# A relative-bias table: spread by DMA through memory before, turned by TensorE matmuls now

## The chip, the core and the metric

One core of one Trainium2 chip runs the whole program. The metric is the time of one execution on the device, in microseconds (us). The kernel before took 2122.17 us (median of three runs, 2119.29 to 2123.08).

## The reference

The reference computes two blocks of layers on 256 tokens and 256 context tokens of width 1024, all in float32. The first block has two layers with attention and a mixture of 32 experts each, the second block a dilated attention and a state-space layer. The change touches only the attention of the first block's second layer, in which 256 tokens stand in a grid of 4 rows of 64 columns, with 16 heads of 64 numbers. A query sees the 4 rows and 16 columns near its own, and gets a bias that depends on the row offset and the column offset:

```python
bias = rel_bias[:, row_off][:, :, col_off].transpose(0, 2, 1, 3)
s_loc = jnp.einsum('bhqd,bhiqjd->bhqij', qr, kw) * C_SCALE + bias
s_ctx = jnp.einsum('bhqd,bhkd->bhqk', qr, kc_h) * C_SCALE
s = jnp.concatenate([s_loc.reshape(B, C_HEADS, GRID_W, n_loc), s_ctx], axis=-1)
p = jax.nn.softmax(s, axis=-1)
```

`rel_bias` holds 16 heads x 15 row offsets x 31 column offsets. The kernel scores every query against all 256 local keys and 256 context keys, and adds a table to the local part: the bias where the key column is in the query's window, and -1e30 where it is not.

## The kernel before

The five engines run one program each, in an order written out by hand, and wait for each other on semaphores. The order of SyncE (SP) is a list, the ring: every weight matrix comes in pieces of 2 MB into five slots of the tile `RG` (with one or two more slots in the tile `AR` while the experts run). SP goes through the list in order, waits until the work that read a slot before is done, and issues the load (L3181). A copy that stands in SP's program ahead of a piece delays that piece.

The stages around the change run so. After the first expert stage the rows come back (`z_load` on ScalarE's queue), VectorE joins them, and `pe_odd_begin` transposes them with matmuls against a diagonal (L2021); ScalarE and VectorE write the transposed and modulated tokens to `HT` (L2041, L2069). Then `pe_odd` projects the first half of the heads: part c=0 is Q (four banks, 256 columns, L2099), part c=1 is K (four banks, 512 columns, L2099), part c=2 is V (four banks, 512 columns, L2101). Each instruction in the program is two MATMUL records in the trace, since float32 goes in two passes. ScalarE empties banks 0 to 3 (L2108, L2110, L2112). After that `odd_done` waits for the last V bank and for the bias table, and the attention begins (L814 are the scores), with the second half of the projection between its units.

The bias table is `BT`, 16 heads x 384 columns on 128 partitions: partition q (and q+64 for the odd grid rows, shifted by 64 columns) is a query column, and the columns are six row offsets x 64 key columns. Partition q needs the table's row read from an offset that falls as q rises, so it can't be loaded with one forward stride. Before, `sp_bias_spread` makes 16 copies from memory to memory, one for each head (L2119), into `OBD` with 64 rows of 448 numbers for each head, each row reversed in its start; they stand in SP's program ahead of piece `("ada", 0, 6)`, in the first layer's projection. Then `sp_bias` loads the two halves of `BT` (L2126) ahead of piece `("odd", 2, 1)`, and VectorE adds the mask `NM` in eight instructions (L2149).

## Time and profile before

| what | value |
|---|---|
| median of 3 runs | 2122.17 us |
| the profiled execution | 2122.17 us |
| its span on the chip | 2120.3 us |
| TensorE (matmul) busy | 1955.7 us, 92% |
| VectorE / ScalarE / GpSimd busy | 647.4 / 370.5 / 322.0 us |
| data moved by DMA | 584.22 MB, mean 276 GB/s |
| chain that ended last | TensorE 65%, DMA 22%, VectorE 5% |

The span is the time between the first and the last instruction of the execution; 1.9 us lie around it. "Busy" says how long an engine had something to do, not that it was waited for. The chain that ended last is followed back from the last instruction, from each to what released it: what stands in it had no slack. A wait that isn't in it costs nothing.

### The profile page before, as it was taken

The numbers are of one execution on the slowest core, as the hardware profiler recorded it, in microseconds if no ns is written. First come the engines' busy times: TensorE is split into PE (matmuls) and PEld (weight loads), VectorE is DVE, ScalarE is ACT, GpSimd is POOL, SyncE is SP. The second block draws the span as 40 slices with busy tenths as digits, with TensorE's granted clock in tenths as the row PEclk, the third lists the DMA queues.
The fourth block names the chain that finished last, engine by engine and source line by source line (L and its number), as shares of the span: only waits on it lengthen the run. The fifth ranks groups of instructions, "written<-read, shape, count | busy, mean of one in ns | idle before, by whom it ended". The sixth has DMA issues, their size and how long they took to land.

```text
span 2120.3 us, 34138 instructions
## 1 busy us (share of the span) xinstructions
PE 1955.7 (92%) x14829; PEld 1223.9 (58%) x14829; DVE 647.4 (31%) x1508; ACT 370.5 (17%) x821; POOL 322.0 (15%) x264
## 2 busy tenths in 40 slices
PE   5999999999999969999999988988879989989998
PEld 4566575555555445546555444444457677665884
DVE  1234382222222232115331111111136031037752
ACT  3133320000000011114310000000021130042131
POOL 0125412000000000115210000000120060040120
PEclk8999999999999999999999999999989999999999
DMA  9563299999999989317399999999964423427221
GB/s 361 151 208 122 88 383 393 427 427 426 427 424 426 427 327 283 111 40 279 140 383 426 426 423 427 426 422 426 393 240 143 146 80 125 153 78 201 81 92 60
DMA packets 131760, 584.22 MB, mean 276 GB/s; under 512 B 19082, under 2 KB 32490, under 8 KB 106896
## 3 DMA queue, kind: packets, MB, share of 16 engines
q1 hardware_dynamic: 113216, 550.26, 66.0%
q10 hardware_dynamic: 12272, 25.26, 3.3%
q0 software_dynamic: 6112, 6.39, 0.9%
q8 instruction: 122, 2.00, 0.4%
q14 instruction: 38, 0.31, 0.0%
HBM read 572.29 MB, written 23.22 MB: 281 GB/s over the span
## 4 chain that ended last, share of the span: by engine, by line
PE 65%; DMA 22%; DVE 5%; issue 3%; POOL 2%; ACT 2%; SPq 1%; POOLq 0%; DVEq 0%; ACTq 0%
DMA RG<-in_moe_w 20%; PE banks L1545 12%; PE banks L2527 8%; PE banks L1570 5%; PE banks L2099 4%; PE banks L2529 4%; PE banks L1093 4%; PE banks L1521 3%; PE banks L684 3%; PE banks L2101 3%; PE banks L2728 3%; PE banks L2939 2%; POOL AR L921 2%; PE banks L814 2%; PE banks L842 1%
## 5 line engine op out<-in xcount | busy, mean ns | idle before, releaser
L1545 PE MATMUL banks<-RG,HT 128*64 128x256 f32 x3616 | 426.6, 389 | 34.6 <-DMA RG<-in_moe_w 32.7
L1545 PEld LDWEIGHTS banks<-RG,HT 128*64 128x64 f32 x3616 | 250.1, 134 | 218.1 <-DMA RG<-in_moe_w 55.0
L1775 POOL DMA_INDIRECT y_rows<-AR x64 | 63.6, 994 | 871.0 <-DVE AR L1584 870.1
L1554 DVE TENSOR_TENSOR AR<-AR,banks 128x256 f32<-128x256 f32 x64 | 38.6, 603 | 484.3 <-ACT AR L1550 433.1
L1570 PE MATMUL banks<-RG,AR 128*64 128x512 f32 x752 | 171.7, 598 | 3.1 <-DVE AR L1563 3.1
L2527 PE MATMUL banks<-HT,RG 128*128 128x256 f32 x768 | 168.0, 380 | 0.8 <-ACT HT L553 0.8
L2527 PEld LDWEIGHTS banks<-HT,RG 128*128 128x128 f32 x768 | 145.4, 190 | 22.8 <-issue 2.4
L1550 ACT ACTIVATE AR<-banks 128x256 f32<-128x256 f32 x64 | 24.5, 383 | 749.9 <-PE banks L1545 749.9
L1521 PE MATMUL banks<-AR 128*128 128x256 bf16 (+1 forms) x1152 | 149.2, 277 | 1.7 <-DVE AR L1509 1.5
L1521 PEld LDWEIGHTS banks<-AR 128*128 128x128 bf16 x1152 | 108.2, 98 | 33.4 <-issue 18.3
L1570 PEld LDWEIGHTS banks<-RG,AR 128*64 128x64 f32 x752 | 49.8, 136 | 93.8 <-issue 83.6
L2099 PE MATMUL banks<-HT,RG 128*128 128x256 f32 (+1 forms) x256 | 84.8, 489 | 3.4 <-ACT HT L2041 1.5
L2529 PE MATMUL banks<-RG,HT 128*128 128x512 f32 x192 | 84.1, 594 | 0.0
L1093 PE MATMUL banks<-RG,HT 128*128 128x512 f32 x192 | 83.3, 594 | 0.8 <-DVE HT L904 0.8
L921 POOL TENSOR_SCALAR AR<-AR,ST 128x768 f32<-128x768 f32 (+1 forms) x24 | 45.0, 1883 | 240.7 <-DVE ST L899 240.1
L342 PE MATMUL banks<-RG,SC 128*32 128x128 f32 x1536 | 51.0, 290 | 23.8 <-DMA RG<-in_ada_w 13.7
L684 PE MATMUL banks<-RG,HT 128*128 128x512 f32 (+1 forms) x192 | 70.7, 531 | 2.3 <-DMA RG<-in_even_w_in 2.3
L921 POOL TENSOR_SCALAR AR<-AR,SVT 128x512 f32<-128x512 f32 x27 | 42.0, 1563 | 193.7 <-DVE SVT L899 193.6
L2099 PEld LDWEIGHTS banks<-HT,RG 128*128 128x128 f32 x256 | 47.9, 190 | 39.6 <-issue 34.9
L1534 ACT ACTIVATE HT<-banks 128x256 f32<-128x256 f32 x128 | 49.0, 383 | 103.8 <-PE banks L1521 103.8
L1545 PE MATMUL banks<-AR,HT 128*64 128x256 f32 x480 | 57.5, 390 | 6.4 <-DMA AR<-in_moe_w 6.4
L1570 PE MATMUL banks<-AR 128*64 128x512 f32 x272 | 62.1, 599 | 1.0 <-DVE AR L1563 1.0
(480 smaller groups left out, 2397.5 us busy)
## 6 DMA issues: line engine op xcount, KB each, us to landing
RG<-in_moe_w SPq DMA_DIRECT2D x160, 2048.0 KB, 23.9
AR<-in_moe_w SPq DMA_DIRECT2D x32, 2048.0 KB, 23.1
RG<-in_ada_w SPq DMA_DIRECT2D x24, 2048.0 KB, 9.3
RG<-in_attn_w_in SPq DMA_DIRECT2D x20, 2048.0 KB, 7.9
RG<-in_odd_w_in SPq DMA_DIRECT2D x6, 2048.0 KB, 20.3
RG<-in_ssm_w_in SPq DMA_DIRECT2D x4, 2048.0 KB, 9.3
AR<-y_rows ACTq DMA_DIRECT2D x6, 1024.0 KB, 7.6
RG<-in_even_w_in SPq DMA_DIRECT2D x2, 2048.0 KB, 23.1
```

Source lines behind the costliest of these rows:

```text
L684: m = pe.matmul(PS[b][:, 0:wd], HT[:, k, 128 * t:128 * t + 128], w[:, k, :], start=k == 0, stop=k == 7)
L921: g.tensor_scalar(u["pb"][x], u["pb"][x], A.small_of(s, 3)[:, x:x + 1], None, MUL).then_inc(*ev("weighed_pool", name, s, x))
L1093: m = pe.matmul(PS[b], HT[:, k, 128 * t:128 * t + 128], w[:, k, :], start=k == 0, stop=k == 7)
L1521: m = pe.matmul(p, E.HB[t][:, i, k, :], E.one_hot(g, t), start=t == 0 and i == 0, stop=t == E.nt - 1 and i == 2)
L1545: m = pe.matmul(p[64 * h:64 * h + 64, 256 * i:256 * i + 256], x[:, k, :], w[:, h, k], start=k == 0, stop=k == 7, skip_group_check=True)
L1570: m = pe.matmul(q[64 * h:64 * h + 64, :], x, w2[:, i, 512 * h:512 * h + 512], start=i == 0, stop=i == 3)
L1775: g.indirect_dma_start(y, off, E.Y[b], None, bounds_check=2047, oob_is_err=False).then_inc(*event)
L2099: m = pe.matmul(p[:, 0:wd], w[:, k, 128 * j:128 * j + 128], HT[:, k, 0:wd], start=k == 0, stop=k == 7)
L2101: m = pe.matmul(p, HT[:, k, 128 * j:128 * j + 128], w[:, k, :], start=k == 0, stop=k == 7)
L2527: m = pe.matmul(p[:, 0:256], w[:, k, 128 * j:128 * j + 128], HT[:, k, 0:256], start=k == 0, stop=k == 7)
L2529: m = pe.matmul(p, HT[:, k, 128 * j:128 * j + 128], w[:, k, :], start=k == 0, stop=k == 7)
L2728: m = pe.matmul(PS[2 * h + t], src[:, k, 128 * t:128 * t + 128], w[:, k, :], start=k == 0, stop=k == 7)
```

## The change

The 16 memory-to-memory copies, the tensor `OBD` and the two loads of `BT` go. In their place the program loads the bias of each head as 64 partitions with a forward stride (`bias_of`), 7 x 64 numbers each, into seven staging buffers `SG`, and reverses the order of the partitions with a matmul against a fixed matrix `R2` (64 rows; twice the reversed identity side by side, so that the result stands on both halves of 128 partitions). There are 16 such matmuls of 448 columns into banks 4 to 7: seven after Q, seven after K, two after V. VectorE adds the mask from the bank into `BT` in two instructions for each head. SP loads `R2` and the first seven heads ahead of the first projection weights, ScalarE the other nine between its evacuations. `DG` and `NM` move to other places in `AR`, and the mask is loaded with 448 columns in place of 384. All lines of the changed program after the first edit stand one or more numbers away from those before.

```diff
@@ -181,7 +181,6 @@
         TBL = [nc.dram_tensor(f"slot_tokens{i}", [64, 32 + n], F).ap() for i, n in enumerate((15, 7))]
         APD = nc.dram_tensor("power_rows", [192, 128], F).ap()
         FRD = nc.dram_tensor("dist_bias", [16, 384], F).ap()
-        OBD = nc.dram_tensor("odd_bias", [16, 64, 448], F).ap()
         KK = 1024
 
         def ar(off, *shape, dt=F):
@@ -1999,7 +1998,7 @@
 
 
 
-        DG = [ar(6 * KK + 128 * t, 128) for t in range(4)]
+        DG = [ar(128 * t, 128) for t in range(4)]
 
         def odd_on_act(t):
             return 6 if t < 2 else 4
@@ -2074,7 +2073,8 @@
         KT1 = ar(12 * KK, 8, 512)
         VV = ar(16 * KK, 4, D)
         BT = ar(0, 16, 384)
-        NM = ar(9 * KK, 384)
+        SG = [ar(6 * KK + 448 * i, 448) for i in range(6)] + [ar(20 * KK, 448)]
+        R2, NM = ar(20 * KK + 448, 128), ar(6 * KK + 3264, 448)
         OX = XS[:, 3, :].rearrange("p (a b) -> p a b", a=4)
 
         def odd_bank(c, hf, j):
@@ -2112,18 +2112,21 @@
                 ins = act.activation(VV[:, j, 512 * hf:512 * hf + 512], p, ACT.Copy)
             ins.then_inc(*ev("odd_out", c, hf, j))
 
-        def sp_bias_spread(sp):
-
-            for h in range(16):
-                src = bass.AP(I["na_bias"].tensor, 465 * h + 139, [[31, 7], [-1, 64], [1, 64]])
-                sp.dma_start(OBD[h].rearrange("q (a b) -> a q b", a=7), src).then_inc(*dm("bias_spread", h))
+        BIAS_LAST = (6, 6, 6, 6, 6, 6, 6, 13, 13, 13, 13, 13, 13, 13, 15, 15)
+
+        def act_bias_load(act, h):
+            act.wait_ge(*at("bias_turned", h - 7))
+            act.dma_start(*bias_of(h)).then_inc(*dm("bias_loads", h))
+
+        def bias_of(h):
+            src = bass.AP(I["na_bias"].tensor, h * 465 + 76, [[1, 64], [31, 7], [1, 64]])
+            return SG[h % 7][0:64].rearrange("p (a b) -> p a b", a=7), src
 
         def sp_bias(sp):
 
-            sp.wait_ge(*at("bias_spread", 15))
-            for x in range(2):
-                src = OBD[:, :, 64 * (1 - x):64 * (1 - x) + 384].rearrange("h q n -> q h n")
-                sp.dma_start(BT[64 * x:64 * x + 64], src).then_inc(*dm("bias_loads", x))
+            sp.dma_start(R2[0:64], K["k_rev2"][0:64]).then_inc(*dm("bias_first", 0))
+            for h in range(7):
+                sp.dma_start(*bias_of(h)).then_inc(*dm("bias_first", 1 + h))
 
         def pe_odd(pe):
             for b in range(2):
@@ -2131,26 +2134,38 @@
             for c in range(3):
                 for j in range(4):
                     pe_odd_part(pe, c, 0, j)
+                for h in range(7 * c, min(7 * c + 7, 16)):
+                    if h < 7:
+                        pe.wait_ge(*at("bias_first", 7))
+                    else:
+                        pe.wait_ge(*at("bias_loads", BIAS_LAST[h]))
+                    if h >= 4:
+                        pe.wait_ge(*at("bias_out", h - 4))
+                    pe.matmul(PS[4 + h % 4][:, 0:448], R2[0:64], SG[h % 7][0:64], start=True,
+                              stop=True).then_inc(*ev("bias_turned", h))
 
         def act_odd(act):
             act.wait_ge(*at("turned", "mix1", 3, 1))
             for p in range(2):
-                act.dma_start(NM[64 * p:64 * p + 64], K["k_nam"].rearrange("p a b -> p (a b)")[:, 0:384]).then_inc(
+                act.dma_start(NM[64 * p:64 * p + 64], K["k_nam"].rearrange("p a b -> p (a b)")[:, 0:448]).then_inc(
                     *dm("bias_tables", p))
             for c in range(3):
                 for j in range(4):
                     act_odd_part(act, c, 0, j)
+                for h in range(7 * c + 7, min(7 * c + 14, 16)):
+                    act_bias_load(act, h)
 
         def dve_odd(v):
             v.wait_ge(*at("bias_tables", 1))
-            v.wait_ge(*at("bias_loads", 1))
-            for h in range(0, 16, 2):
-                b = BT[:, h:h + 2, :]
-                v.tensor_tensor(b, b, bc(NM, 1, 2), ADD).then_inc(*ev("bias_out", h // 2))
+            for h in range(16):
+                b = PS[4 + h % 4]
+                v.wait_ge(*at("bias_turned", h))
+                v.tensor_tensor(BT[0:64, h, :], b[0:64, 64:448], NM[0:64, 64:448], ADD)
+                v.tensor_tensor(BT[64:128, h, :], b[64:128, 0:384], NM[64:128, 0:384], ADD).then_inc(*ev("bias_out", h))
 
         def odd_done(e):
             e.wait_ge(*at("odd_out", 2, 0, 3))
-            e.wait_ge(*at("bias_out", 7))
+            e.wait_ge(*at("bias_out", 15))
 
         SM1 = SVF[:, 512:544].rearrange("p (a b) -> p a b", a=4)
         PB1 = [[ar(6 * KK + 512 * i, 512) for i in range(3)], [ar(7 * KK + 512, 512), ar(8 * KK, 512), SVF[:, 0:512]]]
@@ -3152,14 +3167,10 @@
                     sp.wait_ge(*at(*before[slot]))
                 if i == 4:
                     sp.wait_ge(*at("x_loads", 3))
-                if key == ("ada", 0, 6):
-                    sp_bias_spread(sp)
                 if key == ("ada", 1, 2):
                     sp_overflow(sp, E0)
                 if key == ("odd", 0, 0):
                     sp.wait_ge(*at("z_load3", 0))
-                if key == ("odd", 2, 1):
-                    sp.wait_ge(*at("turned", "mix1", 3, 1))
                     sp_bias(sp)
                 if slot == NS and (key[1] not in begun):
                     l = key[1]
```

How the change moves instructions is shown for two engines. TensorE, from the last bank of Q to the first scores. The rows give line, operation, tiles, shape and the semaphores waited for; `s_ring1` to `s_ring4` are landed weights, `s_act_projected` is ScalarE's evacuation. Before:

```order
L2099 MATMUL banks<-HT,RG 128x256 [waits s_ring1]
L2099 MATMUL banks<-HT,RG 128x256 x7
L2099 MATMUL banks<-HT,RG 128x512 [waits s_act_projected,s_ring2]
...
L2099 MATMUL banks<-HT,RG 128x512 [waits s_act_projected,s_ring2]
L2099 MATMUL banks<-HT,RG 128x512 x7
L2101 MATMUL banks<-RG,HT 128x512 [waits s_act_projected,s_ring3]
...
L2101 MATMUL banks<-RG,HT 128x512 [waits s_act_projected,s_ring3]
L2101 MATMUL banks<-RG,HT 128x512 x7
L814 MATMUL banks<-AR 128x512 [waits s_bias_out,s_act_projected]
```

Now (L2144 is the turning matmul, L813 the scores that were L814):

```order
L2099 MATMUL banks<-HT,RG 128x256 [waits s_ring1]
L2099 MATMUL banks<-HT,RG 128x256 x7
L2144 MATMUL banks<-AR 128x448 [waits s_bias_first] x4
L2144 MATMUL banks<-AR 128x448 [waits s_bias_out,s_bias_first] x3
L2099 MATMUL banks<-HT,RG 128x512 [waits s_act_projected,s_ring2]
...
L2099 MATMUL banks<-HT,RG 128x512 [waits s_act_projected,s_ring2]
L2099 MATMUL banks<-HT,RG 128x512 x7
L2144 MATMUL banks<-AR 128x448 [waits s_bias_out,s_bias_loads] x7
L2101 MATMUL banks<-RG,HT 128x512 [waits s_act_projected,s_ring3]
...
L2101 MATMUL banks<-RG,HT 128x512 x7
L2144 MATMUL banks<-AR 128x448 [waits s_bias_out,s_bias_loads] x2
L813 MATMUL banks<-AR 128x512 [waits s_bias_out,s_act_projected]
```

Seven matmuls have come in after Q, seven after K, and two after V, right ahead of the scores, which wait for the last addition of the mask (`s_bias_out`). No instruction of TensorE has gone.

SP, at the first layer's projection and at the second layer's first weights. Before:

```order
L3181 DMA RG<-in_ada_w 128x8x512 [waits s_ada_rows] x2
L2119 DMA odd_bias<-in_na_bias 7x64x64 [waits s_pe_projected]
L2119 DMA odd_bias<-in_na_bias 7x64x64 x15
L3181 DMA RG<-in_ada_w 128x8x512
...
L3181 DMA RG<-in_odd_w_in 128x8x512 [waits s_z_load3,s_down]
L3181 DMA RG<-in_odd_w_in 128x8x512 [waits s_up_first]
L3181 DMA RG<-in_odd_w_in 128x8x512 [waits s_up]
L3181 DMA RG<-in_odd_w_in 128x8x512 [waits s_ada_rows] x2
L2126 DMA AR<-odd_bias 64x16x384 [waits s_bias_spread,s_pe_turned,s_pe_projected]
L2126 DMA AR<-odd_bias 64x16x384
L3181 DMA RG<-in_odd_w_in 128x8x512
```

Now (L3192 is the load of a ring piece that was L3181):

```order
L3192 DMA RG<-in_ada_w 128x8x512 [waits s_ada_rows] x2
L3192 DMA RG<-in_ada_w 128x8x512 [waits s_pe_projected] x3
...
L2127 DMA AR<-in_k_rev 64x128 [waits s_z_load3,s_down]
L2129 DMA AR<-in_na_bias 64x7x64 x7
L3192 DMA RG<-in_odd_w_in 128x8x512
L3192 DMA RG<-in_odd_w_in 128x8x512 [waits s_up_first]
L3192 DMA RG<-in_odd_w_in 128x8x512 [waits s_up]
L3192 DMA RG<-in_odd_w_in 128x8x512 [waits s_ada_rows] x2
L3192 DMA RG<-in_odd_w_in 128x8x512 [waits s_pe_projected]
```

The 16 copies have gone from between the pieces of `in_ada_w`, the two table loads from ahead of the last projection piece, and eight small loads stand ahead of the first.

On ScalarE seven of the loads (L2119 now) follow the four evacuations of Q (L2108), each behind the turning matmul that frees its staging buffer, and two follow those of K (L2110).

## Rows read from the trace of the kernel before

**Rows 1.** the page: busy time of the engines, and the chain's shares.

```profile
PE 1955.7 (92%) x14829; PEld 1223.9 (58%) x14829; DVE 647.4 (31%) x1508; ACT 370.5 (17%) x821; POOL 322.0 (15%) x264
...
PE 65%; DMA 22%; DVE 5%; issue 3%; POOL 2%; ACT 2%; SPq 1%; POOLq 0%; DVEq 0%; ACTq 0%
```

**Rows 2.** the chain of waits, 760 to 880 us: start, length, what.

```profile
794.50 6.72 ACT HT L2041 x19
...
801.57 0.83 issue
802.40 41.52 PE banks L2099 x128
843.92 27.48 PE banks L2101 x64
871.42 0.61 ACT AR L2112
...
872.07 1.13 PE banks L814 x4
```

**Rows 3.** timeline, 873 to 886 us: start, length, engine, line, tiles [idle before].

```profile
873.35 0.69 DVE L886 TENSOR_REDUCE SVT<-banks 128x2 f32<-128x512 f32 x1 [29.25 <-PE banks L814]
...
877.42 3.69 PE L2099 MATMUL banks<-HT,RG 128*128 128x256 f32 x16 [0.56 <-ACT AR L2108]
...
881.04 1.13 PE L814 MATMUL banks<-AR 64*128 64x512 f32 x4
...
882.10 3.72 PE L2099 MATMUL banks<-HT,RG 128*128 128x256 f32 x16
```

**Rows 4.** line L814: duration ns min/median/max, first and last start, forms.

```profile
L814 PEld LDWEIGHTS banks<-AR x192: 182/186/188, 130.5 to 1880.2; 64*128 64x128 f32 x192
```

**Rows 5.** VectorE groups by shape: count | busy us, mean ns.

```profile
L1554 DVE TENSOR_TENSOR AR<-AR,banks 128x256 f32<-128x256 f32 x64 | 38.6, 603 | 484.3 <-ACT AR L1550 433.1 <-issue 51.2
...
L1194 DVE TENSOR_TENSOR AR<-banks,AR 128x512 f32<-128x512 f32 x8 | 5.5, 690 | 32.4 <-PE banks L1093 32.4
...
L350 DVE TENSOR_TENSOR AR<-banks,AR 128x128 f32<-128x128 f32 x16 | 4.7, 291 | 29.2 <-PE banks L342 29.2
```

**Rows 6.** VectorE, timeline, 837 us: the eight bias additions.

```profile
837.06 7.04 DVE L2149 TENSOR_TENSOR AR<-AR 128x768 f32<-128x768 f32 x8 [34.76 <-DMA AR<-odd_bias]
```

**Rows 7.** the DMA queues' issues on SP, timeline, 60 to 96 us.

```profile
74.65 20.10 SPq L2119 DMA_DIRECT2D odd_bias<-in_na_bias  x16
```

**Rows 8.** the same, 780 to 845 us.

```profile
788.38 16.23 SPq L3181 DMA_DIRECT2D RG<-in_odd_w_in  x5
```

**Rows 9.** issue of in_na_bias copies, ns min/median/max.

```profile
L2119 SPq DMA_DIRECT2D odd_bias<-in_na_bias x16: 727/1213/1922, 74.6 to 93.5; - x16
```

**Rows 10.** issue of the mask's 64-partition copies on ACT, the same columns.

```profile
L2138 ACTq DMA_DIRECT2D AR<-in_k_nam x2: 537/571/605, 800.9 to 801.5; - x2
```

**Rows 11.** DMA issues between 788 and 788.9 us: count, KB, us to landing.

```profile
RG<-in_odd_w_in SPq DMA_DIRECT2D x1, 2048.0 KB, 8.3
```

**Rows 12.** windows: length, busy time of each engine, granted clock, DMA share, GB/s.

```profile
74.65:94.79 20.14, 20.14 (x80) 14.91 (x79) 3.00 (x2) 4.94 (x10) 0.00 (x0) 1.00 0.40 79
94.00:131.50 37.50, 36.48 (x128) 21.22 (x126) 19.54 (x34) 8.96 (x21) 8.15 (x8) 1.00 0.54 178
131.50:200.00 68.50, 62.84 (x822) 46.10 (x820) 36.40 (x89) 31.55 (x89) 39.38 (x32) 1.00 0.57 199
...
770.00:772.00 2.00, 0.00 (x0) 0.00 (x0) 0.00 (x0) 0.00 (x0) 0.45 (x1) 0.56 0.33 109
774.00:776.00 2.00, 1.50 (x30) 1.54 (x34) 0.00 (x0) 0.00 (x0) 0.00 (x0) 0.50 0.27 55
```

**Rows 13.** SP's waits, 990 to 1200 us: total, times, longest.

```profile
SPq L3181 <- PE banks L1545: 77.5, 19, 9.7
SPq L3181 <- PE banks L1093: 51.5, 2, 45.0
```

**Rows 14.** the whole chain: one wait for weights in the second expert stage.

```profile
1170.42 25.74 DMA RG<-in_moe_w
```

## The prediction

> **What bounds the kernel now.** I read the page first: TensorE is busy for 92% of the span, and it holds 65% of the chain that ended last, with DMA at 22% [rows 1]. So work added to TensorE counts in full wherever TensorE itself is the chain, and the question is what the chain is at the place of the change. That is the second view. From 802.40 to 871.42 us the chain is TensorE alone, the twelve projection groups of the first half of the heads without a gap; ahead of them stands ScalarE writing `HT`, behind them one evacuation and the first scores at 872.07 [rows 2]. Nothing of the bias table is in it: VectorE's eight additions ran from 837.06 to 844.1, 28 us before the scores needed them [rows 6]. In the kernel before, the bias table costs the end nothing there.
>
> The third question is whether the copies in the first layer cost something. They held SP's queue for 20.1 us from 74.65 on [rows 7], and the ring pieces behind them came that much later. But TensorE was busy all through that stretch, for 36.48 of 37.50 us to 131.5 and for 62.84 of 68.50 to 200 [rows 12], so at most 6.7 us of idle time can hide behind it.
>
> **What goes.** (1) The 16 copies. SP is free 20 us earlier, and one ring piece comes earlier; the next pieces wait for slots that TensorE frees. TensorE has no late weights to catch up with: I take 0, bounded by 0 and the 6.7 us of idle time just named. (2) The two table loads and the eight additions: 0, since all of it ended 28 us early. This cover is used up by the change, as (6) shows.
>
> **What comes: TensorE.** (3) Sixteen turning matmuls, each two records. 64 records of 512 columns took 27.48 us in the V part [rows 2], 0.429 us each; 448 columns make 0.376. 32 x 0.376 = 12.0 us, and nothing else of TensorE runs beside it. The program has no matmul chain of 64 rows that all sit on the same partitions, so its pace is bounded from both sides by the nearest rows. Below: the scores' four records on 64 rows of two different halves took 1.06 us from start to start of the next kind (881.04 to 882.10) [rows 3], 0.265 each, so 0.232 at 448 columns and 7.4 us in all. Above: if each load of the stationary operand, 186 ns [rows 4], stood bare between the matmuls, 32 x 0.186 = 6.0 us would be added, 18.0 in all. I take 12.0, since the 128-row matmuls of the same type hide that load completely.
>
> The Trainium skill ("TensorE: Matmul & The Clock Gate", Part 3) says that a weight load overlaps matmuls in flight only where the row group differs. By that rule all 32 loads here, on one row group, would be bare and the sum would be 6.0 us larger; the trace's 128-row chain, gapless over 128 records on one row group [rows 2], speaks against it.
>
> (4) The switch between full and 64-row matmuls. Sixteen records of 256 columns should take 16 x 0.219 = 3.51 us (0.219 from 41.52 less 64 x 0.429, over 64) [rows 2], and the scores behind them started 3.62 after (877.42 to 881.04); coming back cost 1.06 - 2 x 0.429 = 0.20 [rows 3]. So 0.3 a visit, and for the first two visits 0.6 us. Between 0 and 1.
>
> (5) Waits inside a group of seven. There are four banks, so matmul h waits for VectorE's addition h-4. From banks, 128 columns took 291 ns and 512 took 690 [rows 5]; 384 come to 0.557, two of them with an issue gap to 1.15 us a head. VectorE starts 0.15 us behind the matmul (873.20 to 873.35) [rows 2, 3]. With matmuls each 0.75 us, head 4 could start at 3.1 us after the group's begin and needs addition 0, done at about 2.15; head 5 at 3.85 needs 3.3; head 6 at 4.6 needs 4.45. No wait, by a small margin: 0. The slower row is 603 ns for 256 columns [rows 5], which scales to 0.90; then head 5 waits 0.85 us and head 6 1.0 more, and the two groups cost 3.7 us.
>
> (6) The tail. The last two turning matmuls stand right ahead of the scores. After the last V matmul: 0.1 for the switch, 0.75 each, the first bank ready at 0.85, VectorE from 1.0 to 2.15 and from 2.15 to 3.3, and the scores at 3.35. Before it was 0.65 (871.42 to 872.07) [rows 2]. 3.35 - 0.65, less the 1.5 already counted in (3), is 1.2 us. With the slow additions it is 1.35 us more. The gap is about 1.7 us of idle TensorE; in the window 770 to 772 us, where it had nothing to do, its granted clock fell to 0.56 on average, and it was 0.50 when work came back [rows 12]. The 0.83 us of idleness at 801.57 [rows 2] cost no clock; I cost this gap at nothing, and at 1 us at most.
>
> **What comes: the queues.** (7) SP issues eight small loads ahead of the first projection piece. Behind them on SP stand all six projection pieces, and TensorE waits for the first. It was issued at 788.38 and landed 8.3 us later [rows 8, 11], at 796.7; TensorE began at 802.40 for ScalarE's sake [rows 2]. That is 5.7 us of cover. Issuing `R2` is like one of the mask's copies, 0.57 us [rows 10]; a bias copy took SP between 0.727 us when the queue was empty and 1.213 as a median [rows 9]. Seven at 0.727 and `R2` make 5.7: the piece lands at 802.4, just in time. Seven at 1.213 make 9.1, so TensorE starts 3.4 us late, after nearly 5 us of idleness, and then the lower clock costs about 1 us more. I take 0.3 of 0 to 4.5, near the lower row: the copies before kept only 0.40 of the 16 DMA engines busy [rows 12], which fits their outermost dimension of 7, and the new loads have 64 there. The first head's data are needed only at 816, and the second piece has 8 us more cover than the first.
>
> The Trainium skill ("DMA: Bandwidth & Descriptors", Why a DMA increments its semaphore by 16 and not by 1) says that such a copy is spread over the largest number of engines up to 16 that divides both outer dimensions: 7 before, 16 now. The share agrees (7/16 = 0.44), and by the rule the new loads drain in less than half the time, so SP's own issue sets the pace (5.7 us); without it the queue would (9.1 us).
>
> (8) ScalarE issues seven loads after Q and two after K. Behind them wait its evacuations of K and V. Seven at 0.727 are 5.1 us from 817 on, and the first K bank is full only at 816.4 + 5.6 + 6.9 = 828.9. Hidden; at 1.213 each still hidden. They land during the 27.5 us of K's matmuls, well before head 7 is turned: 0.
>
> **Does the delay reach the end?** After the projection the chain is TensorE, then the second expert stage, where it runs over waits for weights, such as 25.74 us from 1170.42 [rows 14]. A stream bound by DMA could absorb a late TensorE if its loads were issued independently. They are not: between 990 and 1200 us SP waited 51.5 us for the output projection (L1093) and 77.5 for the experts' own matmuls (L1545) [rows 13]. The stream starts when TensorE frees slots, so it moves with it, and all is passed on.
>
> **Sum.** 12.0 + 0.6 + 0 + 1.2 + 0.3 = 14.1 us. The profiled execution took 2122.2 us, which is also the median of the runs shown, so 2136.3 us.
>
> **Rivals.** (A) VectorE paces the turning: additions at 0.90 us. For: the row of 603 ns. Against: three other rows lie on one line through 0.557. It adds 3.7 + 1.35: 2141.3. (B) Bare weight loads, 6.0 us more: 2142.3; for and against stand in (3). (C) SP's queue is late: the first piece lands 3.4 us late and the clock falls, 4.2 more than I took: 2140.5. For: the median issue; against: the low DMA share. (D) The turning runs at the pace of the scores, 7.4 in place of 12.0: 2131.7. Against: the scores' heads lie on different partitions, these don't. (E) Not slower: the expert stage absorbs the delay. The place is the run of waits for weights from 1170 on, each of some 26 us; if SP's first expert loads ran on a clock of their own, TensorE's 14 us would only shorten these waits, and the time would be 2122.2. It decides from the point where the slots of the first loads are free before TensorE's delayed work; the 51.5 us of waiting for L1093 say they are not. (F) Faster: only if, besides (E), the freed 20 us of SP gave back idle time of the first layer, down to 2115.5 (6.7 less).
>
> **Chances.** My forecast 0.70, A 0.07, B 0.06, C 0.09, D 0.04, E 0.02, F 0.02. About 0.2% (4 us) is what a measurement of this kernel can tell from no change. A to D are all slower by more than that, so slower 0.96, within 0.02, faster 0.02. The range runs from just under D to just over B: 2131 to 2143; the forecast's own is 2134 to 2139.
>
> **What the profile after would show.** (3) 32 records at L2144 with starts 0.376 apart; bare loads would make it 0.56, the paired pace 0.23. (5) No idle time of TensorE that ends with VectorE inside the groups. (6) Scores 3.35 us behind the last V matmul. (7) L2099 beginning within 1 us of ScalarE's last write, with no wait for a DMA. (8) No wait of TensorE for the bias loads. The second expert stage as long as before, shifted. TensorE's time between the joined rows and the scores grown by 14 us. If the expert stage came out shorter by about what the projection is longer, E was right and the forecast wrong; if the first layer's attention were shorter by several us, F.

## The result, and the profile after

The changed kernel took 2151.93 us (median, 2148.38 to 2152.79) against 2122.62 for the kernel before in the same comparison: ratio 1.0138, 95% interval 1.0125 to 1.0151. It is slower by 29 us, where 14 were forecast, and it lies outside the range of 2131 to 2143. In the experiments below it was timed again, on another chip: 2146.73 against 2118.68 (15 runs), ratio 1.0131 (1.0116 to 1.0147), 28.05 us slower. The execution of the kernel before whose rows are shown ahead of the prediction was 3.5 us above that median of 15, and the profiled execution of the changed kernel (span 2144.4 us) is shorter than each of its nine timed ones (the shortest span is 2146.6). So the two traces show a smaller difference (24.1 us) than the medians, and the ledger below counts intervals within each trace.

The page of the changed kernel, busy time and chain; beside them stand [rows 1]:

```profile
span 2144.4 us, 34236 instructions
...
PE 1973.9 (92%) x14861; PEld 1233.5 (58%) x14861; DVE 658.1 (31%) x1532; ACT 371.1 (17%) x821; POOL 321.9 (15%) x264
...
PE 67%; DMA 22%; DVE 3%; issue 3%; POOL 2%; ACT 2%; SPq 1%; ACTq 0%; POOLq 0%; DVEq 0%
```

TensorE has 32 matmul records and 32 weight loads more than before (14861 against 14829), as counted, but 18.2 us more busy time, where 32 x 0.376 is 12.0. The rest is more time for the same work: the records are 0.40 us apart and not 0.376, and some matmuls ran at a lower clock.

The chain of waits of the changed kernel around the change (start, length, what), beside [rows 2]; L2129 are the seven bias loads on SP, L2144 the turning matmuls, L2163 and L2164 VectorE's additions, L813 the scores:

```profile
769.29 3.34 DMA y_rows<-AR
...
774.52 11.85 DMA AR<-y_rows
...
786.44 0.57 SPq L2127
787.05 0.65 SPq L2129
...
791.17 0.63 SPq L2129
791.84 14.23 DMA RG<-in_odd_w_in
806.21 16.51 PE banks L2099 x64
822.72 5.62 PE banks L2144 x14
828.34 27.66 PE banks L2099 x64
856.00 5.55 PE banks L2144 x14
861.56 27.66 PE banks L2101 x64
889.22 0.96 PE banks L2144 x2
890.20 0.55 DVE AR L2163
890.77 0.56 DVE AR L2164
891.36 0.55 DVE AR L2163
891.92 0.57 DVE AR L2164
892.63 1.65 PE banks L813 x4
894.27 4.79 PE banks L2099 x16
899.09 0.39 ACT AR L2108
899.62 3.69 PE banks L2099 x16
```

In [rows 2] ScalarE writing `HT` stood ahead of L2099. Now the chain comes over SP: eight issues, and then a load that takes 14.23 us. Between the last V matmul and the scores two matmuls and four additions have come in. The granted clock tells the rest. Windows of the changed kernel (columns as in [rows 12]):

```profile
786.00:796.00 10.00, 7.54 (x63) 7.00 (x62) 7.98 (x26) 6.03 (x18) 0.00 (x0) 1.00 0.51 93
...
800.00:802.00 2.00, 0.00 (x0) 0.00 (x0) 0.38 (x2) 0.00 (x0) 0.00 (x0) 0.74 1.05 387
802.00:804.00 2.00, 0.00 (x0) 0.00 (x0) 0.00 (x0) 0.00 (x0) 0.00 (x0) 0.50 1.08 364
...
808.00:810.00 2.00, 2.00 (x6) 1.59 (x5) 0.00 (x0) 0.00 (x0) 0.00 (x0) 0.50 1.06 389
810.00:812.00 2.00, 2.00 (x8) 1.63 (x8) 0.00 (x0) 0.00 (x0) 0.00 (x0) 0.70 1.05 386
812.00:814.00 2.00, 2.00 (x11) 1.77 (x10) 0.00 (x0) 0.38 (x1) 0.00 (x0) 1.00 1.05 387
...
890.00:892.00 2.00, 0.92 (x3) 0.19 (x1) 1.74 (x4) 0.00 (x0) 0.00 (x0) 1.00 0.77 230
892.00:894.00 2.00, 1.37 (x4) 0.33 (x4) 0.48 (x1) 0.00 (x0) 0.00 (x0) 0.78 1.05 403
894.00:896.00 2.00, 2.00 (x6) 1.51 (x5) 1.55 (x5) 0.00 (x0) 0.00 (x0) 0.50 1.06 404
896.00:898.00 2.00, 2.00 (x9) 1.68 (x8) 0.27 (x3) 0.00 (x0) 0.00 (x0) 0.87 0.70 272
```

The first of these rows has a counterpart before, ten microseconds from the issue of the same piece on:

```profile
788.00:798.00 10.00, 8.68 (x76) 8.33 (x75) 7.91 (x26) 6.10 (x18) 0.00 (x0) 1.00 0.86 307
```

After 7.2 us of idleness the clock stood at 0.50 (1.2 GHz in place of 2.4) until about 811.2: 6 records in the window from 808, where there are 11 at 1.00. It fell again, for some 3 us, behind the 1.7 us of idleness ahead of the scores.

Far behind the change is something that no step spoke of. The chain of waits in the last stretch, before:

```profile
2050.79 2.25 issue
...
2054.53 1.13 PE banks L3014 x64
...
2056.12 27.91 PE banks L3043 x128
```

and after (L3029 was L3014, L3058 was L3043):

```profile
2070.05 2.25 issue
...
2073.79 0.85 PE banks L3029 x45
2074.64 1.75 issue
2076.39 0.54 PE banks L3029 x19
...
2077.39 29.59 PE banks L3058 x128
```

TensorE stops for 1.75 us within a run of 64 records, waiting for nothing that the profile shows, and the projection behind it takes 29.59 us in place of 27.91. Its clock had fallen:

```profile
2076.00:2078.00 2.00, 1.14 (x21) 0.89 (x22) 0.00 (x0) 1.03 (x2) 0.00 (x0) 0.88 0.22 71
2078.00:2080.00 2.00, 2.00 (x6) 1.53 (x5) 0.00 (x0) 0.63 (x1) 0.00 (x0) 0.50 0.73 244
```

The ledger, from the end of the store of `y_rows` (774.29 before, 769.29 + 3.34 = 772.63 after), in us:

| interval | before | after | more |
|---|---|---|---|
| to the first weights' matmul | 28.11 | 33.58 | 5.5 |
| Q | 14.04 | 16.51 | 2.5 |
| turning heads 0 to 13 | - | 11.17 | 11.2 |
| K and V | 54.96 | 55.32 | 0.4 |
| last V matmul to scores | 0.65 | 3.41 | 2.8 |
| scores to the next group (877.42; 899.62) | 5.35 | 6.99 | 1.6 |
| from there to the last stretch | 1173.37 | 1170.43 | -2.9 |
| last stretch: "issue" row to the end of L3043/L3058 | 33.24 | 36.93 | 3.7 |
| from there to the end of the span | 36.27 | 37.42 | 1.1 |

The seventh row varies between executions whatever the kernel (1170.9 to 1173.8 in the thirteen other traces of this study that have no added work there). It is not a gain of the change: it is 1172.2 us in the mean of the six traces of the kernel before and its variants, and 1172.1 in the nine of the changed kernel and its variants. Without it the rows come to 28.8 us, and the medians differed by 28.05.

### The profile page after: what moved, and what is told of

Same layout as the page of the kernel before. It is cut to its first block, busy times and chain, and to the rows that moved or that the text cites. A ratio compares the mean times of both kernels' runs of the same rounds, so it can differ in the third digit from the quotient of the medians.

```text
span 2144.4 us, 34236 instructions
## 1 busy us (share of the span) xinstructions
PE 1973.9 (92%) x14861; PEld 1233.5 (58%) x14861; DVE 658.1 (31%) x1532; ACT 371.1 (17%) x821; POOL 321.9 (15%) x264
## 4 chain that ended last, share of the span: by engine, by line
PE 67%; DMA 22%; DVE 3%; issue 3%; POOL 2%; ACT 2%; SPq 1%; ACTq 0%; POOLq 0%; DVEq 0%
DMA RG<-in_moe_w 19%; PE banks L1544 13%; PE banks L2542 8%; PE banks L1569 6%; PE banks L2099 4%; PE banks L2544 4%; PE banks L1092 4%; PE banks L1520 3%; PE banks L683 3%; PE banks L2101 3%; PE banks L2743 3%; PE banks L2954 2%; POOL AR L920 2%; PE banks L813 2%; PE banks L341 1%
## 5 line engine op out<-in xcount | busy, mean ns | idle before, releaser
L2099 PE MATMUL banks<-HT,RG 128*128 128x256 f32 (+1 forms) x256 | 88.7, 506 | 9.1 <-DMA RG<-in_odd_w_in 7.2
L2099 PEld LDWEIGHTS banks<-HT,RG 128*128 128x128 f32 x256 | 50.4, 200 | 47.5 <-issue 43.4
L341 PE MATMUL banks<-RG,SC 128*32 128x128 f32 x1536 | 53.2, 298 | 22.0 <-DMA RG<-in_ada_w 12.6
L341 PEld LDWEIGHTS banks<-RG,SC 128*32 128x32 f32 x1536 | 46.8, 121 | 28.3 <-issue 27.4
## 6 DMA issues: line engine op xcount, KB each, us to landing
RG<-in_moe_w SPq DMA_DIRECT2D x160, 2048.0 KB, 24.3
```

The lines of the kernel that those rows point to most:

```text
L341: m = pe.matmul(q[32 * j:32 * j + 32, :], SC[:, k, :], w[:, k, 128 * j:128 * j + 128], start=k == 0, stop=k == 7, skip_group_check=True)
L2099: m = pe.matmul(p[:, 0:wd], w[:, k, 128 * j:128 * j + 128], HT[:, k, 0:wd], start=k == 0, stop=k == 7)
```

## The experiments

All were timed in five rounds, unless it says otherwise, beside the kernel before on the same chip (medians of 2118.7 to 2121.2 us there). "Over before" is the difference of the medians.

**1. The changed kernel again.** No edit.

> The changed kernel once more, beside the others. In its first trace 24.1 us of delay had gathered between the landing of the rows (z_load3) and the second group of the attention's projection, and the span was 24.1 us longer than before, but the median of its runs was 29.3 us above. Theory P (the place is the projection stage alone, the other 5 us are luck of single executions): the stage again costs 24 us and the time is 24 to 29 us above. Rival Q (a second cost elsewhere that the first trace happened to miss): the stage is 24 us and another stretch is some 5 us longer than in the kernel before.

28.05 us over before. Its trace repeats the same rows: first projection matmul 33.56 us after the store, Q 15.57, scores 3.41 after V, a break of 1.65 us after 45 records of L3029. The stage, from the store to the next group, is 24.3 us longer than before, and the last stretch and the end are 4.7 longer: that is rival Q's second cost. The first trace had it too, hidden by its short seventh row. What the lower clock costs differs between the two traces: in Q 2.5 us in the first and 1.5 in this one, in the scores and the group behind them 1.6 and 3.1.

**2. The first weights ahead of the small loads** (SP's eight loads stand behind the first projection piece).

```diff
                 if key == ("odd", 0, 0):
                     sp.wait_ge(*at("z_load3", 0))
+                if key == ("odd", 1, 0):
                     sp_bias(sp)
```

> Undoes one part: SP issues the first projection piece and only then the eight small loads. Theory P-head (the small loads ahead of it made the first piece land 5.7 us later against the rows, and the engine, idle for 7 us, ran the Q part at the lower clock for another 2.5): 8.2 us less than the changed kernel, some 2143.5, and L2099 follows ScalarE's last write as before. Rival (the small loads disturb the pieces wherever they stand, by sharing the DMA engines): the wait moves to the K part or stays, and less than 3 us is won.

2136.77: 18.1 over before (ratio 1.0084, 1.0070 to 1.0098), 10.0 below the changed kernel. In the trace the first matmul came 27.98 us after the store (28.11 in the kernel before) and Q took 14.05. The head (all that comes ahead of the first turning matmul) cost 8 us in the traces, 10 in the medians, and in the traces all of it is the place of the loads.

**3. The tail earlier** (heads 14 and 15 turned between V's second and third bank).

```diff
                 for j in range(4):
                     pe_odd_part(pe, c, 0, j)
-                for h in range(7 * c, min(7 * c + 7, 16)):
...
+                    if j != (3, 3, 1)[c]:
+                        continue
+                    for h in range(7 * c, min(7 * c + 7, 16)):
...
```

> Undoes another part: the last two heads are turned between the second and the third V bank, not ahead of the scores. Theory P-tail (VectorE's last additions kept the scores back, and the gap lowered the clock for them): the gap ahead of the scores falls from 3.4 us after the last V matmul to 0.7, of which 1.5 was matmul work that only moves; so 1.2 us for the wait and 1.6 us for the clock come back, 2.9 us together, and two more switches between full and 64-row matmuls cost nothing new. Rival (the clock falls there for another reason, or the switches cost more than they seem): less than 1.5 us.

2143.71, 3.0 below the changed kernel; the intervals touch (ratio 1.0100 to 1.0131 against 1.0116 to 1.0147), so the time alone doesn't show it. The trace does: the scores began 0.67 us behind the last V matmul again, and they and the group behind them took 5.34 us as in the kernel before, so the clock did not fall there.

**4. Only the copies gone** (the kernel before without the 16 copies; its two table loads read `na_bias` with a forward stride, so the bias values in `BT` are other ones).

```diff
-            sp.wait_ge(*at("bias_spread", 15))
             for x in range(2):
-                src = OBD[:, :, 64 * (1 - x):64 * (1 - x) + 384].rearrange("h q n -> q h n")
+                src = bass.AP(I["na_bias"].tensor, 0, [[1, 64], [465, 16], [1, 384]])
...
-                if key == ("ada", 0, 6):
-                    sp_bias_spread(sp)
```

> The kernel before without the 16 memory-to-memory copies in the first layer; the table is loaded from the bias array in the same shapes but unreversed, so its values are other ones. Theory P (the copies were hidden: 0.0): within 1 us of the kernel before, 2122, with the first layer's attention at the same place relative to its projection. Rival (the copies cost TensorE something in the first layer, and the changed kernel got it back): 1 to 2.6 us faster, as the changed kernel's first attention began 2.6 us earlier in its trace.

2118.94 against 2118.68, ratio 1.0000 (0.9991 to 1.0009). 20 us of SP's time in the first layer were worth nothing.

**5 and 6. Only the matmuls.** The kernel before with 16 matmuls of 448 columns in the places of the turning ones, whose result nobody reads, on 64 rows (5) and on 128 rows (6).

```diff
                 for j in range(4):
                     pe_odd_part(pe, c, 0, j)
+                for h in range(7 * c, min(7 * c + 7, 16)):
+                    pe.matmul(PS[4 + h % 4][:, 0:448], IDN[0:64, :], HT[0:64, 0, 0:448], start=True, stop=True)
```

> The kernel before with the 16 matmuls of 64 rows and 448 columns at the same three places, nothing waiting for them and nothing loaded for them; their result isn't used. Theory P (the turning costs its matmul time, 12.0 us, and 0.3 to 0.4 us for each pair of switches): 12.5 to 13 us above the kernel before, 2135. Rival Q (there is a further cost of delaying TensorE at this place, given out in later stages, that the 24.1 us of the trace don't show): more than 15 us above.

> As the one before, with the full 128 rows in place of 64. Theory (a matmul takes its columns, 448 of them 0.376 us, whatever its rows; the switch between row shapes costs 0.3 us a visit): 12.0 us above the kernel before, 0.5 to 1 us less than with 64 rows. Rival (64-row matmuls on one row group lose something of their own, such as bare weight loads): the full-row form is several us faster.

16.6 over before for 64 rows (ratio 1.0080, 1.0066 to 1.0093), 15.5 for 128 (1.0066, 1.0052 to 1.0079). The first expectation was missed by 3 to 4 us, and the more than 15 of its rival came true; the second was missed by as much. The traces say where: the stage grew by 12.0 and 11.1 us, 14 records taking 5.46 us on 64 rows and 5.26 on 128, and the rest was in the last stretch, 3.6 and 3.8 us longer, with the same break in L3029's counterpart and a projection of 29.6 us. Nothing but TensorE's matmuls had been added here. So the break belongs neither to the loads nor to the new waits.

**7. Only the loads.** The kernel before with the eight small loads ahead of the first projection piece, into the staging buffers, unused; the attention waits until they have landed, and `DG` stands where the change puts it.

```diff
                 if key == ("odd", 0, 0):
                     sp.wait_ge(*at("z_load3", 0))
+                    sp_first(sp)
```

> The kernel before with the eight small loads ahead of the first projection piece, their data unused (the diagonal matrices move as in the changed kernel to make room). Theory P-head: TensorE begins the Q part 5.7 us late and at the lower clock, 8.2 us above the kernel before, 2130.5. Rival (the head delay needs the rest of the change, such as the moved buffers or the missing copies): within 1 us of the kernel before.

2129.08, 9.6 over before (ratio 1.0047, 1.0033 to 1.0060). The trace has the stage 7.3 us longer and the last stretch as before (33.25). The first piece was issued at 795.22 and landed 14.06 us later, as in the changed kernel.

**8. The same bytes in long packets** (the changed kernel, but each of the first seven loads brings 64 rows of 448 numbers that stand in one stretch; seven heads' bias values are other ones).

```diff
-                sp.dma_start(*bias_of(h)).then_inc(*dm("bias_first", 1 + h))
+                src = bass.AP(I["na_bias"].tensor, h * 465 + 76, [[1, 64], [1, 448]])
+                sp.dma_start(SG[h][0:64], src).then_inc(*dm("bias_first", 1 + h))
```

> The changed kernel with the seven first bias loads as 64 rows of 448 numbers in one piece each, in place of 7 pieces of 64: the same bytes and the same eight issues, a seventh of the packets; the bias values of seven heads are other ones. Two theories of the head delay. I (SP's issue: eight times 0.63 us, 5.4 us in all, before the first piece goes out): the first piece still lands about 802 relative to the kernel before, so TensorE's start is late by 0 to 1 us only and the 5.7 us seen were not issue alone. II (the 3136 packets of 256 bytes sit ahead of the piece in the DMA rings): the piece's time from issue to landing falls from 14.2 us to the 8.3 of the kernel before, and 5.9 us and the clock loss come back, some 8 us less than the changed kernel. If the piece still takes 14 us from issue to landing with a seventh of the packets, II is wrong.

> The long-packet kernel once more. Its first profile showed no wait for the first piece and 2136.1 us, but its other runs took 2141.7 to 2145.3. Theory (the piece lands so near to the time at which it is needed that single runs fall on either side, and late ones also lose the clock): runs on both sides again, 2136 and 2141 to 2145, and a slow one's profile, if it is one, shows the wait. Rival (the first profile was luck of another stage): the profile shows no wait in a slow run.

2143.17 (2136.13 to 2145.26), and in the repetition with three rounds 2141.61 (2134.41 to 2144.99): 23.7 and 22.7 over before, 4.4 and 5.4 less than the changed kernel's 28.05. In the first trace (the run of 2136.13) the piece was issued at 791.04 and TensorE began L2099 at 800.01, behind VectorE's last write of `HT` and without a wait for the piece, and Q took 14.05; in the second (the run of 2144.99) the piece, issued at 792.38, landed 10.02 later and Q took 15.74. DMA traffic in 16 us, first the changed kernel (786 to 802), then experiment 8's second trace (the same), then the kernel before (788 to 804):

```profile
DMA packets 4416, 3.06 MB, mean 191 GB/s; under 512 B 3278, under 2 KB 3342, under 8 KB 4416
```

```profile
DMA packets 2130, 3.93 MB, mean 245 GB/s; under 512 B 161, under 2 KB 673, under 8 KB 2129
```

```profile
DMA packets 2653, 5.38 MB, mean 337 GB/s; under 512 B 34, under 2 KB 34, under 8 KB 2652
```

3136 packets of 256 bytes (7 heads x 64 rows x 7) against 448 of 1792 bytes. That is what differs: the same bytes and issues, in fewer and longer packets. With the long ones TensorE starts 0 to 1.0 us late instead of 5.5, but the 5.1 us of issuing stay. In the two traces 8 and 5.3 of the head's 8 us come back, in the medians about half of the 10 that experiment 2 gained. So the packets are the larger part of the head in the traces, and SP's issue time takes away the slack that would have covered it.

The first trace shows one thing more. It has the same gap ahead of the scores as the changed kernel, and the clock did not fall behind it (granted clock 1.00 throughout; the scores took 1.13 us and the group behind them 3.67):

```profile
883.97 1.13 PE L813 MATMUL banks<-AR 64*128 64x512 f32 x4 [1.71 <-DVE AR L2165]
```

Seven traces of this study have that gap of 1.71 us. The scores and the group behind them took 1.5 to 1.6 us longer than before in five of them, 3.1 in experiment 1 and nothing here.

**9. Sixteen tiny matmuls elsewhere** (the kernel before, 16 matmuls of 16 columns behind the second expert stage, where TensorE is idle).

> The kernel before with 16 more matmuls of 16 columns, unused, in the 9 us in which TensorE waits for the rows after the second expert stage: instructions, but no time on the path. What is disputed: the profiles of all kernels with 16 more matmuls (the changed one and the two with matmuls alone) took 81 to 82 us for the last stretch, where the kernels without them took 77.5, and TensorE stops there for 1.6 us inside a run of 64 small matmuls beside an instruction fetch, and runs at the lower clock after it. Theory F (the number of instructions ahead of that place shifts it against the blocks in which instructions are fetched): the last stretch is again 81 to 82 us and the time 3.5 to 4.5 us above the kernel before. Rival T (the stop comes from the shifted time or from the work in the projection): within 1 us of the kernel before.

2121.99 against 2118.94, ratio 1.0018 (1.0009 to 1.0027): 3.05 us for work that no one waits for. Its last stretch took 36.83 us (33.24 before), and shows why (timeline; L3016 is L3014):

```profile
2050.29 0.96 PE L3016 MATMUL banks<-AR 128*32 128x63 f32 x51 [1.14 <-POOL AR L3002]
2052.88 0.42 PE L3016 MATMUL banks<-AR 128*32 128x63 f32 x13 [1.64 <-issue]
```

**10 and 11. The changed kernel with 48 tiny matmuls** at that same place (10), and with the mends of 2 and 3 as well (11).

```diff
+            for _ in range(48):
+                pe.matmul(PS[3][:, 0:16], IDN[:], IDN[:, 0:16], start=True, stop=True, skip_group_check=True)
```

> The changed kernel with 48 such matmuls at that place. A block is 16 KB in the trace; if an instruction is 64 bytes and a float32 matmul four of them, a block is 64 matmuls, and 16 + 48 restore the alignment of the kernel before. Theory F: the last stretch is 77.5 us again and the time 3.5 to 4.5 us below the changed kernel, so 24 above the kernel before. Rival T: as slow as the changed kernel or up to 1 us slower.

> The changed kernel with the first piece issued ahead of the small loads, the last two heads turned between the V banks, and the 48 small matmuls. If head (10.0), tail (3.0) and alignment (4) are separate terms, it is 17 below the changed kernel and 11.5 to 12.5 above the kernel before, which is the turning matmuls alone; no version with them on this path beats the kernel before. Rival (the terms overlap, one hides in another): 3 us or more above that.

Both missed: 2154.3 and 2144.27, 35.4 and 25.3 over before. The break in the last stretch was gone (33.25 and 33.24 us), but the 96 records did not fit into the gap:

```profile
1570.31 20.55 PE L2309 MATMUL banks<-IDN 128*128 128x16 f32 x96 [3.83 <-DMA y_rows<-AR]
```

They took 0.21 us each, at a granted clock of 0.50, and the first weights' matmul of the dilated attention came 32.8 us behind the store of `y_rows`, where it came 21.8 behind it in the changed kernel. Their times therefore prove nothing about the break; they led to the last three.

**12 to 14. Both mends; both mends with 48 tiny matmuls where TensorE waits for weights; the changed kernel with the 48 alone.** The tiny ones stand in the second expert stage, three ahead of each of 16 matmuls.

```diff
                 if h >= 1:
                     pe.wait_ge(*at("dist_out", h - 1))
+                for _ in range(3):
+                    pe.matmul(PS[4][:, 256:272], IDN[:], IDN[:, 0:16], start=True, stop=True, skip_group_check=True)
                 pe.matmul(PS[4][:, 256:512], REV[:], STG[:, h % 8, :], start=True, stop=True,
```

> The changed kernel with both mends: the first projection weights issued ahead of the eight small loads, and heads 14 and 15 turned before the last half of V's banks. If head and tail are separate terms of the sum, the gains add: 10.0 and 3.0, so 13.0 below the changed kernel, 15 above the kernel before (range 13.5 to 16.5). If they are one and the same (a clock that falls anyway, somewhere in the stage), 10 below and 18 above. The last stretch should still have its stall and take 82 us, since the number of instructions is the changed kernel's.

> The same, and 48 tiny matmuls (16 columns) added in the second expert stage, three ahead of each of the 16 matmuls that turn the distance bias there, where TensorE waits for weights. If the stall of the last stretch hangs on how many instructions TensorE has executed, it goes as it did in the two runs that added 48 elsewhere (78.5 us in place of 82): 12 to 12.5 above the kernel before, which is the sixteen turning matmuls and the switches alone. If the stall belongs to the added work, the same as the kernel without the 48: 15.

> The changed kernel with the same 48 tiny matmuls in the second expert stage and nothing else. By the count of instructions: 3.5 to 4.5 us below the changed kernel, so 23.5 to 24.5 above the kernel before, and the last stretch 78.5 us. By the rival, that any added work of TensorE in the attention causes the stall: no difference to the changed kernel (28 above) and 82 us. Should the tiny matmuls cost time in the expert stage, that stage would be longer than 552 us; three of them take about 0.2 to 0.6 us, against waits for weights of some 7 us for each expert, so I expect nothing.

| kernel | us (lowest to highest) | over before | ratio, 95% | stage over before | last stretch |
|---|---|---|---|---|---|
| both mends | 2138.96 (2136.83-2142.88) | 17.8 | 1.0087 (1.0070-1.0104) | 13.3 | 36.97 |
| both, and 48 | 2135.72 (2134.24-2140.48) | 14.5 | 1.0073 (1.0058-1.0088) | 13.3 | 33.25 |
| changed, and 48 | 2148.44 (2146.75-2151.23) | 27.2 | 1.0131 (1.0115-1.0147) | 23.3 | 33.25 |

"Stage" and "last stretch" are the ledger's intervals in the traces. The chain of waits of experiment 13:

```profile
2062.85 2.25 issue
...
2066.60 1.13 PE banks L3033 x64
...
2068.19 27.91 PE banks L3062 x128
```

and of experiment 12 at the same place:

```profile
2066.52 0.85 PE banks L3031 x45
2067.37 1.80 issue
2069.17 0.54 PE banks L3031 x19
```

The traces decide: with 48 more matmuls of TensorE, and nothing taken away, the break is gone in 10, 11, 13 and 14, and 3.6 to 3.7 us with it. The rival, that any added work causes it, has fallen. The tiny matmuls cost nothing where they stand now: the stretch from the stage to the last one took 1172.0 and 1173.5 us, within what the other traces have. In the medians experiment 13 shows it (3.3 less than 12, though the intervals overlap); 14 does not, 27.2 against 28.05 with intervals of some 3 us each, so its time alone tells nothing. Head and tail are additive in the traces: the mends took 8.1 and 2.3 us off the stage alone and 10.6 together. In the medians both together gave 10.3, less than the 13.0 expected (17.8 over before, where 15 was forecast).

No kernel here beats the kernel before. With everything mended (experiment 13) the turning is still 14.5 us slower than the copies, which cost nothing.

## Why the prediction was wrong, step by step

**(1), (2) right.** Experiment 4: 0.

**(3), (4) right.** 16 matmuls in three visits took 5.62 + 5.55 + 1.70 us in experiment 12, 12.9 with the switches, against 12.6 forecast. Rival B and rival D are out: 14 records would have taken 7.9 us with bare loads and 3.3 at the paired pace. The turning matmuls of the changed kernel, weight loads and matmuls:

```profile
L2144 PEld LDWEIGHTS banks<-AR x32: 182/187/187, 822.6 to 890.0; 64*128 64x128 f32 x32
L2144 PE MATMUL banks<-AR x32: 536/536/640, 822.6 to 890.4; 64*128 64x448 f32 x32
```

The loads last 187 ns, as in [rows 4], yet 14 of these matmuls take 5.55 to 5.62 us, 0.40 each with the switch. The Trainium skill's rule ("TensorE: Matmul & The Clock Gate", Part 3), that a weight load overlaps only matmuls of another row group, would have made it 0.56 each; these matmuls are all on one row group, and the measurement decides against it. The records come every 0.39 to 0.40 us, though, and not every 0.376: in experiment 6 14 records on 128 rows took 5.26 us, as forecast, and on 64 rows 5.46, so a small cost of the 64-row form or of its switches is left, and these runs don't tell the two apart.

**(5) right.** VectorE took 550 and 560 ns for the two additions (forecast 557), and no wait of TensorE stands in the groups. Rival A is out.

**(6) half right.** The scores came 3.41 us behind V, forecast 3.35. But the gap of 1.7 us brought the clock down to 0.50, and the scores and the group behind them took 1.6 us longer; I had costed that at nothing, and at 1 us at most. The row that I went by was an idle time of 0.83 us, half as long. In experiment 12, without the gap, these 1.6 us are gone. Their size is not fixed: the same gap cost 3.1 us in experiment 1's trace and nothing in experiment 8's first, so "nothing" can happen, and was the exception.

**(7) failed, and is most of the miss.** It was costed at 0.3 of 0 to 4.5, and the ledger has 5.5 + 2.5 = 8.0. The issues were as forecast: 0.57 and seven at 0.63 to 0.69, 5.4 us in all. What failed is "the piece lands at 802.4": I added the 8.3 us from issue to landing of [rows 11], measured with no other load ahead on SP, to a piece that now stood behind 3136 packets of 256 bytes. It took 14.23. For 10 us the DMA engines moved 93 GB/s (786 to 796), where they moved 307 before (788 to 798). I had asked how long SP is busy, and how many engines carry the loads, but not how many packets they are. Rival C named the place and priced it by the wrong quantity, the median issue time; its 3.4 us late and 1 us of clock were 5.5 and 2.5 (1.5 to 2.5 over all traces with a late piece). Experiments 2 and 7 show that the loads' place is the cause, experiment 8 that the packets are more of it than the issuing.

The Trainium skill ("DMA: Bandwidth & Descriptors", Why small descriptors are slow) gives a 256-byte descriptor 11 cycles in place of 8. As an estimate from that figure, 0.8 MB at the 380 GB/s of the weights would take 2.1 us in long packets and 2.9 in short ones, and these 0.8 us more do not come near the 5.9 us that the piece took longer to land; the trace decides.

**(8) right.** TensorE never waited for the nine loads of ScalarE.

**"All is passed on" right.** The stage grew by 24 us in the traces, the 14.1 of the forecast and some 10 beside it, and all of it reached the end: the rest of the way to the last stretch took 1172.2 us in the mean before and 1172.1 after. Rival E is out.

**What no step had.** The break of the last stretch, 3.7 us with its clock: in every kernel with 16 more matmuls of TensorE, in none with loads alone, gone again with 48 more. It was not in the prediction at all, and it is 3.7 of the 14.7 us that it missed. And 1.1 us between VectorE's last write and the end of the span: 4.2 to 4.3 us in all traces of the changed kernel and its variants, 3.1 to 3.2 in before and in experiments 4 to 7 and 9. No run tells its cause, which stays open.

Put together, 14.1 = 11.1 (heads 0 to 13) + 2.7 (the tail with its two matmuls) + 0.3 (the head) became 28.8 = 11.2 + 2.8 + 8.0, and four terms that I had at nothing: the clock behind the tail 1.6, K and V 0.4, the last stretch 3.7, the end 1.1.

## What to carry to other kernels

A load's time from issue to landing holds only for the queue in which it was measured: before putting loads ahead of it, count their packets, not only their bytes and issues. An idle gap of TensorE can cost more than its length: in six of the seven traces with the gap of 1.7 us ahead of the scores the clock fell behind it, for 1.5 to 3.1 us more. And an added matmul can cost time 1200 us later, in a place that has nothing to do with it; a control that adds only the instructions, at a harmless place, tells that apart from the change.

## What the runs showed of the hardware that was not expected

- TensorE's break of 1.5 to 1.9 us with no wait, in the midst of 64 equal records, came and went with the number of instructions executed before: it is in all ten traces with 16 more matmuls and in none of the seven with none or 64 more. It stands behind record 45 in the changed kernel and its variants, and behind record 51 in the kernel before with 16 more matmuls. 16 matmuls are 64 instructions of TensorE here (32 matmuls and 32 weight loads, page), 64 matmuls 256. The queue that the profile calls "instruction" moves packets of 16 KB (122 with 2.00 MB in all, page), and one of them came near the break, here between 2073.5 and 2075.5 us in the changed kernel (in fact within 0.25 us of the start of the 64 records at 2073.79, so 0.6 to 0.85 us ahead of the break):

```profile
q8 instruction: 1, 0.02, 3.2%
```

  The Trainium skill ("Advanced Engine Details and Errata", ISA Cache) says that instructions are cached in lines of 16 KB, 256 instructions each. That fits: 16 matmuls shift the boundary of a line by a quarter, 64 put it back. That the break depends on the count is shown; that it is a late fetch is an inference, since the kernel before has such a packet about there too (0.25 to 0.5 us behind the start of the same 64 records), without a break.
- Tiny matmuls are not cheap at the low clock: 96 records of 16 columns took 20.5 us, 0.21 us each.
- 14 records of 64 rows took 5.46 to 5.62 us, 14 of 128 rows in experiment 6 took 5.26: half the rows save nothing, and on 64 rows the K and V groups behind them took 27.66 us in place of 27.47.
